# In the units behind a two-step unit, the second gated product and both turns stand one block product later

## The reference, cut to what matters

```python
def _swiglu(x, w_gate, w_up, w_down):
    return (jax.nn.silu(x @ w_gate) * (x @ w_up)) @ w_down
```

## Time and profile before

| | |
|---|---|
| time, median of 3 runs | 1314.9 us (1314.81 to 1314.91) |
| time of the profiled execution | 1314.64 us |
| span of the profiled execution | 1312.8 us |
| PE busy | 1298.3 us, 99% of the span |
| DVE busy | 1080.2 us, 82% |
| ACT busy | 791.2 us, 60% |

### The profile page before, as it was taken

The page is one execution under the profiler, slowest core; times in us unless marked ns, Lnnn a source line. Parts: engine busy times, 40 slices in busy tenths (PEclk is TensorE's granted clock), DMA queues, the critical chain, the costliest instruction groups (busy, mean ns, idle before and its releaser), DMA issues.

```text
span 1312.8 us, 19267 instructions
## 1 busy us (share of the span) xinstructions
PE 1298.3 (99%) x7299; PEld 1109.5 (85%) x7300; DVE 1080.2 (82%) x1306; ACT 791.2 (60%) x1038; POOL 140.0 (11%) x212
## 2 busy tenths in 40 slices
PE   9999999999999999999999999999999999999997
PEld 6978999998878889977888888878889988887886
DVE  6977876677999874577999979999876988999985
ACT  6674655555666645585576655666646854566661
POOL 5420000000000100183000000000000001100000
PEclk9999999999999999999999999999999999999999
DMA  9535766665698766515689868598755434779860
GB/s 318 170 107 167 241 192 192 190 206 216 204 319 271 199 222 207 188 24 193 209 257 282 271 204 299 161 326 281 201 184 181 158 100 153 285 214 310 279 183 33
DMA packets 160785, 275.53 MB, mean 210 GB/s; under 512 B 7297, under 2 KB 105874, under 8 KB 156610
## 3 DMA queue, kind: packets, MB, share of 16 engines
q1 hardware_dynamic: 150512, 226.51, 50.0%
q0 software_dynamic: 9904, 46.85, 16.0%
q10 hardware_dynamic: 290, 1.11, 0.2%
HBM read 238.24 MB, written 1.07 MB: 182 GB/s over the span
## 4 chain that ended last, share of the span: by engine, by line
PE 92%; DVE 5%; issue 2%; ACT 1%; DVEq 0%; POOL 0%; ACTq 0%
PE ps L912 18%; PE ps L914 18%; PE ps L913 18%; PE ps L734 6%; PE ps L736 6%; PE ps L735 6%; PE ps L935 3%; PE ps L936 2%; PE ps L942 2%; DVE wlo L681 2%; PE ps L3157 1%; PE ps L1922 1%; PE ps L1095 1%; PE ps L1902 1%; PE ps L1936 1%
## 5 line engine op out<-in xcount | busy, mean ns | idle before, releaser
L642 DVE TENSOR_TENSOR wlo<-raw,whi 128x1024 fp32r<-128x1024 f32 x230 | 273.7, 1224 | 45.6 <-ACT whi L632 44.4
L670 ACT ACTIVATE whi<-arena 128x2048 fp32r<-128x2048 f32 x112 | 214.6, 1916 | 98.4 <-PE ps L914 95.8
L632 ACT ACTIVATE whi<-raw 128x1024 fp32r<-128x1024 f32 x230 | 232.2, 1053 | 63.5 <-PE ps L914 45.7
L681 DVE TENSOR_TENSOR wlo<-arena,whi 128x2048 fp32r<-128x2048 f32 x112 | 255.8, 2287 | 13.8 <-ACT whi L670 12.8
L912 PE MATMUL ps<-whi,ahi 128*128 128x512 f32 x456 | 180.7, 396 | 0.0
L914 PE MATMUL ps<-wlo,ahi 128*128 128x512 f32 x456 | 177.7, 390 | 0.0
L913 PE MATMUL ps<-whi,alo 128*128 128x512 f32 x456 | 177.7, 390 | 0.0
L734 PE MATMUL ps<-ahi,whi 128*128 128x256 f32 x624 | 177.2, 284 | 0.0
L736 PE MATMUL ps<-ahi,wlo 128*128 128x256 f32 x624 | 176.6, 283 | 0.0
L735 PE MATMUL ps<-alo,whi 128*128 128x256 f32 x624 | 176.6, 283 | 0.0
L734 PEld LDWEIGHTS ps<-ahi,whi 128*128 128x128 f32 x624 | 119.7, 192 | 0.9 <-issue 0.3
(11 more groups left out here) (457 smaller groups left out, 2404.4 us busy)
## 6 DMA issues: line engine op xcount, KB each, us to landing
raw<-ffn_w_down SPq DMA_DIRECT2D x88, 512.0 KB, 10.0
arena<-ffn_w_gate SPq DMA_DIRECT2D x32, 1024.0 KB, 8.5
arena<-ffn_w_up SPq DMA_DIRECT2D x32, 1024.0 KB, 8.1
arena<-arena POOLq DMA_DIRECT2D x32, 1024.0 KB, 7.8
raw<-w_up SPq DMA_DIRECT2D x44, 512.0 KB, 4.6
raw<-ffn_w_gate SPq DMA_DIRECT2D x24, 512.0 KB, 4.7
raw<-ffn_w_up SPq DMA_DIRECT2D x24, 512.0 KB, 6.0
raw<-w_down SPq DMA_DIRECT2D x22, 512.0 KB, 4.1
```

The lines of the kernel that those rows point to most:

```text
L632: act.activation(split_half(w_slots(slot)[0], mode), raw_half(h), ACT.Copy).then_inc(hi_ready, 1)
L642: dve.tensor_tensor(lo, raw_half(h), hi.bitcast(F32), ALU.subtract).then_inc(lo_ready, 1)
L670: act.activation(hi, src, ACT.Copy).then_inc(hi_ready, 2)
L681: dve.tensor_tensor(lo, src, hi.bitcast(F32), ALU.subtract).then_inc(lo_ready, 2)
```

## The change

On PE, `t1` now comes ahead of the first turn, and `t2` ahead of the second. On ACT, the high part of `b22` and `snap_y` come ahead of the first turn, and `snap_z` ahead of the second; `snap_y` waits for the second gated product of the unit before, which reads `v5`. On DVE, the sum L1453 comes ahead of the first turn's low part. At the end of a unit that is followed by a two-step unit, the low part of the following `t1` is made ahead of the second gated product. The number of instructions on the engines' arithmetic doesn't change.

```diff
@@ pe_ffn, double
                     product("b21", block(0, 1), r, True, True)
+                    product("t1", block_sum(1), 1, True, True)
                     pe.wait_ge(gated_ready, done + 2)
                     turn(pair_step(before, 0), range(NT))
-                    product("t1", block_sum(1), 1, True, True)
+                    pe.wait_ge(snap_ready, 3 * d + 1)
+                    product("t2", block_sum(2), z, False, True)
                     pe.wait_ge(g_ready, turns + before.steps[0] + 1)
                     turn(pair_step(before, 1), range(NT))
-                    pe.wait_ge(snap_ready, 3 * d + 1)
-                    product("t2", block_sum(2), z, False, True)
                     pe.wait_ge(snap_ready, 3 * d + 2)
                     product("b22", block_sum(4), 1, False, True)
@@ act_ffn, double
                 def snap_y():
                     act.wait_ge(half_done, g.at["t1"] + 2)
+                    if before.double:
+                        act.wait_ge(gated_ready, mult_count(n) + 2 * i)
                     act.activation(v5, ps[:, 1, :], ACT.Copy).then_inc(snap_ready, 1)
                 if before.double:
                     act_block(act, n, c + 3)
-                    turned((0, 1), turns + before.steps[0] + 1)
                     act_block(act, n, c + 4)
                     snap_y()
-                    turned((0, 1), turns + before.steps[1] + 1, last_ghi)
+                    turned((0, 1), turns + before.steps[0] + 1)
                     act_block(act, n, c + 5)
                     snap_z()
+                    turned((0, 1), turns + before.steps[1] + 1, last_ghi)
@@ dve_ffn, double
-                if before.double:
-                    dve_block(dve, n, c + 3)
+                if not before.double:
                     turned((0, 1), turns + before.steps[0] + 1)
-                else:
-                    turned((0, 1), turns + before.steps[0] + 1)
-                    dve_block(dve, n, c + 3)
+                dve_block(dve, n, c + 3)
                 dve.wait_ge(snap_ready, 3 * d + 1)
                 dve.wait_ge(half_done, g.at["b21"] + 2)
                 dve.tensor_tensor(g.v1, r, g.v1, ALU.add).then_inc(c_ready, 1)
+                if before.double:
+                    turned((0, 1), turns + before.steps[0] + 1)
                 dve_block(dve, n, c + 4)
@@ dve_ffn, end of double
+                if following.double:
+                    dve_block(dve, n, c + 9 + downs)
                 dve.wait_ge(silu_ready, silus + 2 * i + 2)
                 dve.wait_ge(c_ready, 2 * d + 2)
                 dve.tensor_tensor(g1, g1, v5, ALU.mult).then_inc(gated_ready, 1)
-                dve_block(dve, n, c + 9 + downs)
+                if not following.double:
+                    dve_block(dve, n, c + 9 + downs)
```

## The result

The changed kernel takes 1329.25 us (median of 5 runs, 1329.07 to 1329.58) against 1314.81 us (5 runs, 1314.48 to 1314.91) of the kernel before: 14.4 us more, ratio 1.011, 95% interval 1.0098 to 1.0121. The forecast was 1328.8.

A forecast was written before the change was run, and what follows sets the result against it. PE was taken to bound the kernel, busy 99% of the span. 8 x 1.19 + 4 x 1.09 = 13.9 us more gave 1328.8 us; forecast range 1326.3 to 1330.5, with rival A 1322.5 to 1331.0.

The forecast's parts named there:

- PE's order by itself: On PE: same products and transposes, so no cost; it only moves the first turn's start 2.72 us later.
- The first turn's low part and what is queued behind it: On DVE: `b22`'s low part, queued behind the turn's, comes late and PE stalls 0.70 us ahead of `b22`.
- The second stall: Ahead of `t3` on PE: its low part, queued on DVE behind the second turn's, comes 0.35 us late.
- The price of a plain restart: On PE: a product behind a stall without a turn takes 2.86 us instead of 2.72, 0.14 more.
- The unit's sum: From the end of `b21` to the end of `t3`: +1.19 us in 8 later units, +1.09 in 4 first ones.
- The second gated product: At a unit's end: behind `t1`'s low part it is free in units 4 and 5; unit 3's wait becomes 0.89 us.
- Loads and clock: Moved loads of the next unit stay hidden, and the granted clock stays at 1.00; nothing added for either.
- Rival A: Only `b22` is late and `t3`'s low part is in time: +8.0 us, 1322.9 us; chance 0.09.
- B: Both low parts arrive in time, so the cover holds and nothing changes: 1314.5 us; chance 0.05.
- C: In unit 3 `t1`'s low part is ready when PE leaves `b21`, cover holds: -4.5 us, 1310.4 us; chance 0.03.
- D: The clock falls, halving the rate of the product behind a stall in 12 units: +46.5 us, 1361 us; chance 0.02.
- E: A load that L689 waits for comes late in 8 units: +4 us, 1332.8 us; chance 0.05.

The follow-up runs named there:

- experiment 1: The changed kernel with DVE making the low part of `b22` ahead of the first turn's and that of `t3` ahead of the second turn's; 1315.48 us.
- experiment 3: The changed kernel with only the low part of `b22` made ahead of the first turn's low part on DVE; 1330.39 us.
- experiment 8: The changed kernel with PE's wait for `snap_y` moved ahead of the second turn and a fulfilled wait put directly ahead of `t1`'s wait; 1329.85 us.
- experiment 5: The changed kernel with the old end of a unit, the second gated product ahead of the following `t1`'s low part; 1332.20 us.
- experiment 2: The changed kernel with only the low part of `t3` made ahead of the second turn's low part on DVE; 1324.15 us.
- experiment 4: The kernel before with PE's new order alone, ACT and DVE keeping their old orders; 1346.84 us.
- experiment 6: The kernel before with only the new end of a unit, the following `t1`'s low part ahead of the second gated product; 1318.59 us.

## Why the prediction was right, step by step

- **PE's order by itself costs nothing.** Shown by experiment 1 for units 4 and 5, which take 11.85 us on average against 11.86. In unit 3 the second turn then waits 0.14 us for the first turn's low part.
- **The first turn's low part and what is queued behind it.** Forecast 0.70 us of stall ahead of `b22`; measured 1.14 - 0.35 = 0.79. The end of ACT's copy of the turn came where it was forecast, 1.28 us behind the turn's start (404.61 - 403.33) for a forecast of 1.29 (403.68 - 402.39). What was mis-sized is the step from DVE to PE, 0.05 taken from `t1`, 0.15 measured at `b22`.
- **The second stall.** Forecast 0.35; `b22` ends at 410.27 + 0.23 = 410.50, and `t3` starts at 410.90: 0.40. The low part of `t3` ended 4.21 us behind the second turn's start, as forecast (410.76 - 406.55, and 409.81 - 405.60); the step to PE was again 0.14 instead of 0.05, and `b22` ended 0.04 later than forecast.
- **The price of a plain restart.** Taken as 0.14 on a product of 2.72; measured 413.74 - 410.90 = 2.84, so 0.12. `b22` took 410.50 - 407.69 = 2.81 instead of 2.86.
- **The unit's sum.** Forecast +1.19 and +1.09, measured +1.27 and +1.17; 13.9 us in all against 14.4 (14.7 over the units). By the prediction's own timeline, too, the start of `t3` hangs on the second turn and not on `b22` (experiments 3 and 8), so of the step that was too small only the one ahead of `t3` counts, 0.09 us in each unit, and the one ahead of `b22` is absorbed. The upper end of the range added 0.07 at each of 24 hand-overs from ACT to DVE: only the 12 ahead of `t3` could have lengthened a unit in that way, and that hand-over took 0.03 to 0.04 us (404.61 to 404.65, 407.84 to 407.87). The miss of 0.5 us lies inside the range, but in another step than the one for which it was widened.
- **The second gated product.** Free in later units, 0.89 us of wait in unit 3 (measured 0.90), and worth 2.4 us against the old end of the unit, as the units of experiment 5 show.
- **Loads and clock.** L689 of the next unit starts at 420.35 in the changed kernel, directly behind the operation ahead of it, and none of the 16 rows of L689 has idle time ahead of it, so no load was late. The granted clock stayed at 1.00 from 350 to 1100 us, the stretch that holds 9 of the 12 units: the row that the prediction set against the Trainium skill's "TensorE: Matmul & The Clock Gate" decided rightly, and 24 more short stalls brought no swing of the clock.
- **Rival A** had nearly the right price for the second stall alone, 5.9 us (6.2 over the units of experiment 2). Its mirror image, the first stall alone taken away, would by the same sum have given some 10 us, and gives nothing (experiment 3). **B** needed the first turn's high part 0.70 us earlier; it came where it was forecast, and about that time was reached only with another order on DVE (experiment 1). **C** to **E** didn't occur: `t1` of unit 3 starts 0.90 behind `b21`, the clock stayed, and no load was late.

That the in-order list behind the turn is the cause is shown from both sides: moving two instructions on DVE ahead of the hand-over takes the whole loss away, and leaving ACT's high part, `snap_y` and DVE's sum behind the turn as well (experiment 4) raises it from 14.7 to 31.7 us, 2.4 of them by the old end of the unit. In experiments 5 and 6 the units account for 2.4 us of the 2.8 and 3.5 of the 3.6; the rest lies outside them. No version here beat the kernel before; experiment 1 is equal to it. The wait of 0.9 us ahead of `t1` in unit 3 remains in both, with `t1`'s low part directly behind L695 on DVE; I tried nothing against it.

## What to carry to other kernels

When a piece of work is moved later on one engine, go through the in-order list of every engine that handles its result and look at what stands behind the hand-over there: that work becomes late, not the moved piece. Put ready work for the next product ahead of a step that has to wait. Two stalls in a chain aren't added up one by one: removing the earlier one may only feed the later one, so compute the timeline to its end before fixing either.

## What the runs showed that I had not expected

A wait that has long been fulfilled is not free for PE when it stands directly ahead of the wait that binds: the product's first weight load then starts 0.11 to 0.12 us behind the releasing operation instead of 0.05 to 0.06, at `b22` and `t3` of the changed kernel and, moved on purpose, at `t1`. At the product itself 0.03 us of that comes back, since the step from the first to the second matmul shrinks from 0.33 to 0.30 us at the same time. At `b22` it costs nothing here, because `t3` waits for something else in any case; at `t1` of unit 3 it costs the unit 0.05 to 0.09 us. And PE's busy time on the page rose by 5.7 us although its instructions stayed the same: with modelled, overlapping ends of matmuls, short stalls look partly like work.
